# The output projection of a hybrid encoder layer, by halves of its columns instead of tile by tile

## What is computed

```python
h = rms_norm(x, norm_mix_w)
z = h @ w_in                                   # q, k, v, gate, pooled columns
ret = retention(q, k, v) * ret_norm_w * silu(g)
pool = pool_mixer(p, w_pool, pool_scale)
x = x + concatenate([ret, pool]) @ w_out       # the output projection
h2 = rms_norm(x, norm_ffn_w)
logits = h2 @ w_router + b_router
top_vals, top_idx = top_k(logits, 4); gates = softmax(top_vals)
# each expert e, on the tokens that chose it:
gu = xblk @ w_gu[e] + b_gu[e]                  # 1024 -> 2048
act = min(glu, 7) * sigmoid(1.702 * glu) * (clip(lin, -7, 7) + 1)
y = act @ w_down[e] + b_down[e]                # 1024 -> 1024
x = x + sum of gates * y;  y = rms_norm(x, norm_final_w)
```

## Time and profile before

| | |
|---|---|
| time, median of 3 runs | 1267.36 us (1266.95 to 1268.4) |
| time of the profiled execution | 1267.78 us |
| its span | 1266.0 us, 1.78 us less than its time |
| busy PE / DVE / ACT / POOL | 92% / 89% / 73% / 40% of the span |
| projection and routing, first to last PE record | 154.4 to 230.3 us |
| expert stage | from about 233 us to about 1235 us |

### The profile page before, as it was taken

The page is one execution under the profiler, slowest core; times in us unless marked ns, Lnnn a source line. Parts: engine busy times, 40 slices in busy tenths (PEclk is TensorE's granted clock), DMA queues, the critical chain, the costliest instruction groups (busy, mean ns, idle before and its releaser), DMA issues.

```text
span 1266.0 us, 39786 instructions
## 1 busy us (share of the span) xinstructions
PE 1160.1 (92%) x17462; PEld 894.8 (71%) x17463; DVE 1128.3 (89%) x849; ACT 924.4 (73%) x819; POOL 509.2 (40%) x69
## 2 busy tenths in 40 slices
PE   5999999789999999999999999999999999999984
PEld 2455544777777777777777777777888777777741
DVE  5742454789999999999999999999999999999988
ACT  5332432579888888888888888888888888888852
POOL 0120300006666666666665551111166666622400
PEclk9999999799999999999999999999999999999998
DMA  9609331699999999999999999999999999999986
GB/s 350 218 20 353 126 134 58 229 371 378 420 416 416 418 413 417 418 418 417 416 417 414 419 418 418 414 418 413 415 416 419 417 411 420 418 412 409 418 324 255
DMA packets 73254, 458.07 MB, mean 362 GB/s; under 512 B 10076, under 2 KB 10588, under 8 KB 23632
## 3 DMA queue, kind: packets, MB, share of 16 engines
q1 hardware_dynamic: 68480, 445.30, 86.5%
q0 software_dynamic: 3472, 8.21, 1.7%
q10 hardware_dynamic: 1152, 2.19, 0.5%
HBM read 443.26 MB, written 24.77 MB: 370 GB/s over the span
## 4 chain that ended last, share of the span: by engine, by line
PE 44%; DVE 29%; issue 17%; DMA 6%; ACT 2%; DVEq 0%; SPq 0%; ACTq 0%; POOLq 0%
DVE ring L399 20%; PE ps L420 15%; PE ps L456 10%; PE ps L1093 8%; PE ps L1194 4%; PE ps L413 3%; DMA ring<-in_w_down_dram 2%; DMA arena<-in_w_down_dram 1%; DVE arena L492 1%; ACT ring L396 1%; DVE arena L486 1%; DVE arena L489 1%; DMA ring<-in_w_gu_dram 1%; DVE arena L501 1%; DVE arena L495 1%
## 5 line engine op out<-in xcount | busy, mean ns | idle before, releaser
L478 POOL DMA_INDIRECT planes<-arena,slot_row x31 | 484.2, 15619 | 586.8 <-ACT arena L508 586.8
L399 DVE SCALAR_TENSOR_TENSOR ring<-ring 128x2048 f16<-128x2048 f32 x290 | 657.5, 2315 | 15.0 <-ACT ring L396 14.7
L396 ACT ACTIVATE ring<-ring 128x2048 f16<-128x2048 f32 x290 | 543.1, 1905 | 46.4 <-DMA ring<-in_w_gu_dram 22.9
L420 PE MATMUL ps<-arena,ring 128*128 128x88 f16 x12288 | 505.1, 205 | 46.2 <-issue 27.8
L420 PEld LDWEIGHTS ps<-arena,ring 128*128 128x128 f16 x12288 | 489.2, 100 | 55.9 <-issue 43.2
L456 PE MATMUL ps<-ring,arena 128*88 128x512 f16 x1536 | 338.0, 379 | 5.6 <-DVE arena L501 2.6
L456 PEld LDWEIGHTS ps<-ring,arena 128*88 128x88 f16 x1536 | 181.4, 120 | 148.6 <-issue 6.0
L399 DVE SCALAR_TENSOR_TENSOR ring<-arena,ring 128x2048 f16<-128x2048 f32 x94 | 214.4, 2316 | 0.9 <-ACT ring L396 0.9
L396 ACT ACTIVATE ring<-arena 128x2048 f16<-128x2048 f32 x94 | 178.0, 1904 | 12.4 <-DMA arena<-in_w_down_dram 6.5
L413 PE MATMUL ps<-arena 128*128 128x88 f16 x2048 | 94.2, 207 | 10.9 <-issue 7.6
L413 PEld LDWEIGHTS ps<-arena 128*128 128x128 f16 x2048 | 86.6, 101 | 12.0 <-issue 11.9
(11 more groups left out here) (153 smaller groups left out, 592.7 us busy)
## 6 DMA issues: line engine op xcount, KB each, us to landing
ring<-in_w_gu_dram SPq DMA_DIRECT2D x194, 1024.0 KB, 11.9
ring<-in_w_down_dram SPq DMA_DIRECT2D x96, 1024.0 KB, 12.1
arena<-in_w_gu_dram SPq DMA_DIRECT2D x62, 1024.0 KB, 12.5
arena<-in_w_down_dram SPq DMA_DIRECT2D x32, 1024.0 KB, 11.7
ring<-in_w_in_dram SPq DMA_DIRECT2D x4, 2048.0 KB, 12.4
ring<-planes SPq DMA_DIRECT2D x6, 1024.0 KB, 10.1
ring<-in_w_out_dram SPq DMA_DIRECT2D x2, 2048.0 KB, 8.5
arena<-in_x_dram SPq DMA_DIRECT2D x4, 512.0 KB, 11.6
```

What stands on the lines that cost most here:

```text
L396: return act.activation(split_of(slot)[:, 0, :], raw(r), ACT.Copy, scale=SCALE_W)
L399: return dve.scalar_tensor_tensor(split_of(slot)[:, 1, :], raw(r), SCALE_W, split_of(slot)[:, 0, :], ALU.mult, ALU.subtract)
L420: mm = pe.matmul(o, w[:, i, cols], src[:, j, k, :], start=start and n == 0, stop=stop and n == 2, skip_group_check=True)
L478: return pool.indirect_dma_start(out=planes, out_offset=bass.IndirectOffsetOnAxis(ap=rows, axis=0), in_=y_row[0:SCAT, :], in_offset=None, ...
```

## The change

`w_out` is loaded by halves of its columns (512 each) instead of by halves of its rows: columns 0 to 511 into ring slots 4 and 5, columns 512 to 1023 into slots 6 and 7. `project(m)` now takes t = m % 4 and half = m // 4: PE does the first half of all four tiles, then the second half. So slots 4 and 5 are free after the fourth product, and SP issues the loads of chunks 4 and 5 when `out_done` is 4 instead of 8. The split of these two chunks by ACT still waits for `out_done` 8, since it is written to slots 6 and 7. As each tile is complete only in the second half, the steps that follow it are put in another order on PE, ACT and DVE.

```diff
-        def wout(k):
-            j = (k + 4) % 8
-            return ring[:, 4 + j // 2, (j % 2) * D:(j % 2 + 1) * D]
+        def wout(half):
+            return ring[:, 4 + 2 * half:6 + 2 * half, :].rearrange("p s (a c) -> p (s a) c", a=KD // 2)
...
             sp.wait_ge(win_low, 5)
-            sp.dma_start(ring[:, 4:6, :].rearrange("p s (a c) -> p (s a) c", a=2),
-                         w_out[0, W:2 * W, :].rearrange("(k p) c -> p k c", p=P)).then_inc(wout_loaded[1], 16)
+            sp.dma_start(wout(0), w_out[0, :, 0:512].rearrange("(k p) c -> p k c", p=P)).then_inc(wout_loaded[0], 16)
             sp.wait_ge(z_done, 12)
-            sp.dma_start(ring[:, 6:8, :].rearrange("p s (a c) -> p (s a) c", a=2),
-                         w_out[0, 0:W, :].rearrange("(k p) c -> p k c", p=P)).then_inc(wout_loaded[0], 16)
+            sp.dma_start(wout(1), w_out[0, :, 512:1024].rearrange("(k p) c -> p k c", p=P)).then_inc(wout_loaded[1], 16)
...
-            sp.wait_ge(out_done, 8)
+            sp.wait_ge(out_done, NT)
             early(4)
             early(5)
...
             for t in range(NT):
                 norm2(t)
+                if t >= 1:
+                    turned_h2(t - 1)
                 high_part(t)
-                if t == NT - 1:
-                    first_high(4)
-                turned_h2(t)
...
+            first_high(4)
+            turned_h2(NT - 1)
             first_high(5)
...
             for t in range(NT):
-                project(2 * t)
+                project(t)
+            for t in range(NT):
+                project(NT + t)
+                if t >= 2:
+                    route(t - 2)
                 if t >= 1:
                     turn_h2(t - 1)
-                project(2 * t + 1)
-                if t >= 1:
-                    route(t - 1)
+            route(2)
             turn_h2(3)
             route(3)
...
             for t in range(NT):
+                residual(t, 0)
+            for t in range(NT):
                 if t == NT - 1:
                     dve.memset(late[64:P, :], 0.0)
...
-                residual(t)
+                residual(t, 1)
                 normed(t)
                 low_part(t)
-                if t >= 1:
-                    choose(t - 1)
+                if t >= 2:
+                    choose(t - 2)
+            choose(2)
             low(0, 0, DN_CH + 4)
             choose(3)
             low(0, 0, DN_CH + 5)
```

More of the change, by code:

```diff
@@ L1183, in _ @@
                 emptied(pe, ("mix", h))
-            for c in range(2):
-                pe.wait_ge(wout_loaded[c], 16)
             def project(m):
-                t, half = m // 2, m % 2
+                t, half = m % NT, m // NT
+                if t == 0:
+                    pe.wait_ge(wout_loaded[half], 16)
                 take(pe, ("out", m))
@@ L1194, in project @@
                     mm = pe.matmul(bank(("out", m)), mixT[:, k, t * P:(t + 1) * P],
-                                   wout(k)[:, half * 512:(half + 1) * 512], start=(k == 0), stop=(k == KD - 1))
+                                   wout(half)[:, k, :], start=(k == 0), stop=(k == KD - 1))
                 mm.then_inc(out_done, 1)
@@ L1526, in _, with residual @@
             pooled(3)
-            def residual(t):
-                for half in range(2):
-                    m = 2 * t + half
-                    dve.wait_ge(out_done, m + 1)
-                    xs = x_sb[:, t, half * 512:(half + 1) * 512]
-                    ins = dve.tensor_tensor(xs, bank(("out", m)), xs, ALU.add)
-                    free(ins, ("out", m))
-                for half in range(2):
-                    emptied(dve, ("out", 2 * t + half))
-                dve.sem_inc(x2_ready, 1)
+            def residual(t, half):
+                m = NT * half + t
+                dve.wait_ge(out_done, m + 1)
+                xs = x_sb[:, t, half * 512:(half + 1) * 512]
+                ins = dve.tensor_tensor(xs, bank(("out", m)), xs, ALU.add)
+                free(ins, ("out", m))
+                if half:
+                    emptied(dve, ("out", t))
+                    emptied(dve, ("out", m))
+                    dve.sem_inc(x2_ready, 1)
             def normed(t):
```

## The result

The changed kernel takes 1272.99 us (median of 5 runs, 1271.62 to 1273.73), the one before 1266.95 us in the same comparison. The ratio is 1.0045, with a 95% interval from 1.0031 to 1.0058: slower by 5.7 us on the mean of the runs (the two medians lie 6.0 apart). The profiled execution took 1271.62 us, the shortest of the five; its span is 1269.8 us.

What follows compares the result with a forecast made beforehand. The prediction took the chain from projection to first gather as the bound, with no DVE slack behind it. The late `route(2)` and PE's low clock summed to +5.2 on 1267.36, so 1272.6 us; forecast range 1271.5 to 1273.8, wider range 1268.6 to 1274.2.

Steps and rivals of the forecast that it cites:

- The last product ends at 212.8, DVE adds it at 215.8, the last `low_part` stays.: Projection's end: products end some 2.7 us earlier, but DVE's bias split loses that; chain unchanged within 0.1 us.
- `route(2)` starts at 222.9, released by `choose(1)`.: Behind the last `low_part`: `route(2)` needs bank 6, freed by `choose(1)`'s first operation; PE pauses 7.5 us.
- PE at 1.2 GHz through both routings: PE before the gather: low clock after the pause, each `route` 3.64 us instead of 1.70, `turn_h2(3)` 1.9.
- The sum of +5.2: Chain to the gather: `choose(3)` starts at 233.0 instead of 227.76, and the gather at 238.9.
- The rule against the trace: PE's clock behind the wait: the skill's rule could lift it before `route(3)`; the trace's low clock was chosen.
- the second rival: PE from `route(2)` to the gathers: the clock rises inside the stretch, -0.9 to +3.5 us; chance 0.20.
- Loads and layout at nothing: Chunks 4 and 5 issued earlier, and `w_out` in 2 KB rows: both worth or costing 0.
- without cover: Loads of `w_out` with 2 KB rows: would cost 4 us if not hidden in 90 us of other work.
- The delay goes through to the end: Expert stage: DVE has no slack there, so whatever moves the first gather (233.61) moves the end by as much.
- The range of the forecast: First rival, low clock through both routings, +5.2 with bounds on turn and gather: 1271.5 to 1273.8 us; chance 0.58.
- The fourth rival: Last tile: DVE finishes its 12.2 us in under 9.4, gaining up to 2.7 us: 1264.7 us; chance 0.05.
- the third (absorbed): Start of the expert stage: ACT or a landing sets the pace, not the gather; 1267.4 within 0.2%; chance 0.12.

Runs made afterwards that it cites:

- the other bank: The changed kernel with the logits of odd tiles in bank 7 and those of even tiles in bank 6: 1269.11 us, ratio 1.0014.
- The filled pause: The changed kernel with eight matmuls that nobody reads put in PE's pause before `route(2)`: 1270.89 us, ratio 1.0027.
- the better tail: The changed kernel with two logit banks, the bias split early and another order of ACT and DVE behind the last product: 1264.56 us, ratio 0.9975.
- SP's new order: The better tail, with SP issuing stores and loads of chunks 12 and 13 ahead of chunks 10 and 11: 1263.57 us, ratio 0.9972.
- the last experiment: The changed kernel with eight small matmuls (128x32) that nobody reads, on PE between the ranks and the gather: 1274.73 us, ratio 1.0056.

## Why the prediction was right

By its own steps:

- *The last product ends at 212.8, DVE adds it at 215.8, the last `low_part` stays.* Measured 212.81, 215.85 and 221.38 (221.29 in the earlier trace rows). That DVE eats the 2.7 us was shown by moving the bias split: 2.82 us at the gather, 3.1 in the time.
- *`route(2)` starts at 222.9, released by `choose(1)`.* Measured 222.97, with DVE as the releaser; the other bank released it at 219.24.
- *PE at 1.2 GHz through both routings.* `route(2)` 3.60 us, `turn_h2(3)` 1.95 (1.9 taken), the copies at 228.36 (228.2), `route(3)` 229.55 (229.4), `choose(3)` 233.18 (233.0), the gather 239.07 (238.9). The sum of +5.2 at `choose(3)` was +5.42. The filled pause shows that 4.2 us come back at the gather with the full clock.
- *The rule against the trace.* The Trainium skill (TensorE: Matmul & The Clock Gate, "What's actually happening") lets activity release the clock. Here `route(2)` and `turn_h2(3)` ran from 222.97 to 228.3 without a pause, more than the earlier trace rows could show, and the granted clock stayed 0.50; it rose only 3.6 us after the gather's start. Here the row decided, and the second rival fell.
- *Loads and layout at nothing.* Both measured alone: 1.0042 beside 1.0045, and 0.9996. The size put on the layout "without cover", 4 us from the row of `w_in`, was wrong though: the loads by halves of the columns took 8.5 us, no longer than before. It did not enter the sum.
- *The delay goes through to the end.* It does on the mean of the runs, 5.7 us beside 5.46 at the gather. But the reason given, that the stage has no slack, rests on the earlier trace rows, which begin at 290 us. Between the gather and 290 DVE had gaps: 6.34 us busy of 10 from 240 to 250, 5.68 of 10 from 270 to 280 in the kernel before. The profiled execution is only 3.84 us longer. I had no term for PE's pauses without a releaser, so it is in part luck that the mean agrees within 0.5 us.
- *The range of the forecast.* Its terms end at +6.2 us, which is 1273.6 and not 1273.8; nothing hangs on it.

Where the profiled execution lost a part of the delay can be read. DVE's splits of the chunks were 5.44 us late up to 273 us and 4.04 from 281 on, as was the gather for expert 2 (280.75 against 276.71). DVE waits there for ACT, and ACT for that gather; ACT's row in the kernel before and in the changed one:

```profile
278.17 0.76 ACT L468 ACTIVATE arena<-ps 128x704 f16<-128x704 f32 x1 [7.01 <-PE ps L413]
```

```profile
282.20 0.76 ACT L467 ACTIVATE arena<-ps 128x704 f16<-128x704 f32 x1 [6.30 <-PE ps L412]
```

So up to 280 us PE's pauses still count, and on the way to that gather PE had pauses without a releaser of 0.56 and 1.40 us in the kernel before and none in the changed one, which instead ran at a granted clock of 0.50 from about 266.6 to 270.0. The splits were 5.4 us late again by 890 us and 3.8 us by 1212; no row says why. PE's pauses fit the spread of about 1 us around the medians, but that is argued from single traces.

The fourth rival (a faster kernel) did not come, but the experiments show its mechanism to be real once the bias split and the order behind it are out of the way: that is the gain of the better tail. A part of the third (absorbed), 1.4 us of 5.5, did come in the profiled execution, at ACT's wait for the gather and not at a landing.

What stays open is why the clock of the better tail fell during `route(2)`'s short wait, while with SP's new order it held through `route(2)`, and what exactly the pauses without a releaser are. The profile gives them no cause.

## What to carry to other kernels

- When work is regrouped so that results come later together, look at each buffer that goes round between two engines: one bank that served one tile at a time made PE wait 7.4 us here as soon as two tiles' results were due behind each other. Then read what that pause does to PE's clock; a full clock gave back 4.2 of 5.5 us.
- An earlier load is worth only what its reader does sooner. Here the reader did not move, and 34 us of earlier issue gave nothing; an earlier product gave nothing either while its adder was busy with something that could have been done in idle time.
- A list of steps written for one order of the products can hold up another, on an engine that the change does not seem to touch (ACT's copies, with the clock that fell in the wait for them: the products ended 8 us late).

## What I had not expected of the hardware

- Filling PE's pauses with work that nobody reads was worth more than it cost, even with pauses of only 1.2 to 2.1 us: 3.2 us of 1263.57.
- PE's idle time without a releaser in the expert stage differed between traces of nearly the same program (34.5 to 42.9 us without added matmuls), and what of it lay before 300 us went with the time from the gather to the end. A profiled execution should be compared with another only after these pauses are added up in both.
- PE's clock fell in one kernel during a pause of 1.22 us (at about 216.4, from the mean of 0.61 in the window from 216 to 218), and in one with the same pause only at about 218.6, while PE was at work again. It did not rise in 5.3 us of routing and transposing without a pause (222.97 to 228.3 in the changed kernel). In the last experiment the ranks and small float32 matmuls kept PE busy from 235.2 up to the gather, where the changed kernel had a pause of 3.34 us, and the clock rose at about 242.2 instead of 242.7: hardly sooner, for 3.6 us of such work more.
